# Down projections of a hybrid encoder: 16 of 22 row groups by a seven-product scheme, with the weights' split moved from POOL to ACT, DVE and POOL

## The reference

```python
def conv_ffn(x, w_up, conv_w, conv_b, w_down):
    hdn = x @ w_up                              # 1024 -> 2 x 2816
    hdn = causal_dwconv(hdn, conv_w, conv_b)    # 3 taps
    val, gate = jnp.split(hdn, [D_FF], axis=-1)
    return (jax.nn.gelu(gate) * val) @ w_down   # 2816 -> 1024
...
ff = conv_ffn(x, f_w_up[i], f_conv_w[i], f_conv_b[i], f_w_down[i])
x = layer_norm(ALPHA * x + ff, ln2_g[i], ln2_b[i])
```

## Time and profile before

| what | value |
|---|---|
| median of 3 runs (lowest to highest) | 1255.85 us (1255.59 to 1255.90) |
| span of the profiled execution | 1254.0 us |
| PE, PEld | 1246.9 us (99%), 1016.7 us (81%) |
| POOL, DVE, ACT | 861.5 us (69%), 551.0 us (44%), 410.2 us (33%) |
| loads of w_down | 44 of 512 KB, on SP's queue |
| down in layer 0 | from 500.75 us |

### The profile page before, as it was taken

How to read it: one execution, slowest core, us unless ns; L and a number is a source line. 1 busy time by engine, 2 the same in 40 slices (tenths; PEclk the granted TensorE clock), 3 DMA queues, 4 the chain that set the end, 5 groups by cost and what they waited for, 6 DMA issues and landing times.

```text
span 1254.0 us, 17715 instructions
## 1 busy us (share of the span) xinstructions
PE 1246.9 (99%) x5829; PEld 1016.7 (81%) x5829; DVE 551.0 (44%) x880; ACT 410.2 (33%) x684; POOL 861.5 (69%) x1154
## 2 busy tenths in 40 slices
PE   9999999999999999999999999999999999999998
PEld 6887777788888888888888778888888888888887
DVE  6556556564443444410444374364444443201352
ACT  4445444123434333100144484114343434100041
POOL 7555467629888777776577557929887787767573
PEclk9999999999999999999999999999999999999999
DMA  5221233303322233433143222312323224333221
GB/s 197 69 67 67 67 117 101 101 17 107 110 87 99 100 128 90 118 101 101 67 168 101 85 67 84 132 37 101 102 99 100 100 90 128 118 101 98 70 93 59
DMA packets 57292, 120.61 MB, mean 96 GB/s; under 512 B 3760, under 2 KB 36080, under 8 KB 56736
## 3 DMA queue, kind: packets, MB, share of 16 engines
q1 hardware_dynamic: 56192, 117.45, 28.8%
q10 hardware_dynamic: 1056, 2.58, 0.6%
HBM read 117.83 MB, written 2.20 MB: 96 GB/s over the span
## 4 chain that ended last, share of the span: by engine, by line
PE 97%; ACT 1%; DVE 1%; DMA 1%; issue 0%; DVEq 0%; ACTq 0%; SPq 0%
PE bank L439 19%; PE bank L440 19%; PE bank L441 19%; PE bank L458 9%; PE bank L459 8%; PE bank L460 8%; PE bank L735 2%; PE bank L740 2%; PE bank L733 2%; PE bank L554 1%; PE bank L541 1%; PE bank L467 1%; PE bank L525 1%; PE bank L523 1%; PE bank L909 1%; PE bank L910 1%
## 5 line engine op out<-in xcount | busy, mean ns | idle before, releaser
L425 POOL TENSOR_TENSOR w_lo<-stage,w_hi 128x256 fp32r<-128x256 f32 x800 | 593.8, 773 | 29.5 <-issue 1.5
L419 POOL TENSOR_SCALAR w_hi<-stage 128x1024 fp32r<-128x1024 f32 x200 | 213.8, 1069 | 172.8 <-PE bank L460 74.5
L439 PE MATMUL bank<-x_hi,w_hi 128*128 128x512 f32 (+1 forms) x712 | 275.7, 387 | 0.0
L441 PE MATMUL bank<-x_hi,w_lo 128*128 128x512 f32 (+1 forms) x712 | 275.3, 387 | 0.0
L440 PE MATMUL bank<-x_lo,w_hi 128*128 128x512 f32 (+1 forms) x712 | 275.3, 387 | 0.0
L439 PEld LDWEIGHTS bank<-x_hi,w_hi 128*128 128x128 f32 x712 | 133.7, 188 | 27.3
L441 PEld LDWEIGHTS bank<-x_hi,w_lo 128*128 128x128 f32 x712 | 133.7, 188 | 27.2
L440 PEld LDWEIGHTS bank<-x_lo,w_hi 128*128 128x128 f32 x712 | 133.7, 188 | 26.8
L1139 DVE SCALAR_TENSOR_TENSOR tmp<-bank,cols,tmp 128x511 f32<-128x511 f32 x88 | 66.0, 750 | 201.0 <-ACT tmp L1436 190.0
L458 PE MATMUL bank<-w_hi,h_hi 128*128 128x512 f32 x352 | 137.3, 390 | 0.0
L459 PE MATMUL bank<-w_lo,h_hi 128*128 128x512 f32 x352 | 137.0, 389 | 0.0
(11 more groups left out here) (180 smaller groups left out, 1804.6 us busy)
## 6 DMA issues: line engine op xcount, KB each, us to landing
stage<-w_square SPq DMA_DIRECT2D x163, 512.0 KB, 3.3
stage<-w_down SPq DMA_DIRECT2D x44, 512.0 KB, 3.7
rows<-norm_rows SPq DMA_DIRECT2D x4, 1024.0 KB, 5.7
outT<-x SPq DMA_DIRECT2D x7, 256.0 KB, 2.0
x<-xT SPq DMA_DIRECT2D x3, 512.0 KB, 6.8
p_in<-pT ACTq DMA_DIRECT2D x2, 512.0 KB, 3.2
w_ai<-w_lru SPq DMA_DIRECT2D x1, 1024.0 KB, 8.9
stage<-w_square ACTq DMA_DIRECT2D x1, 512.0 KB, 7.1
```

The costliest lines, as they stand in the source:

```text
L419: whole = pool.tensor_scalar(high[:, s, :], stage[:, s, :], 1.0, 0.0, ALU.mult, ALU.add)
L425: piece = pool.tensor_tensor(low[:, s, to], stage[:, s, to], high[:, s, to].bitcast(F32), ALU.subtract)
L439: pe.matmul(out, w_hi[:, s, c:c + P], m_hi, start=first, stop=False)
L441: return pe.matmul(out, w_lo[:, s, c:c + P], m_hi, start=False, stop=last)
```

## The change

`h` and the down weights are cut into 2 x 2 blocks: two halves of the tokens, pairs of row groups, two halves of the outputs. For 8 pairs (row groups 0 to 15) the four block products per output block (8 in all) are replaced by Strassen's scheme in the form with seven: three products in a first pass, four in a second, each over sums and differences of blocks. Row groups 16 to 21 go as before.

- **Sides of h** (DVE, in up): for rounds 0 to 7 the product of gelu and value goes to `folded`, with four sums per pair (`fold_sides`). In down ACT writes a side's high part (`side_top`), DVE its low part (`side_low`), 768 columns in a first-pass step and 1024 in a second-pass step, into three places (`JIT`).
- **Weights**: every unit of the 16 groups is loaded in both passes, through six places of `stage` (two of them on the dead `x_hi` and `x_lo`). DVE makes the sums in place (`first_sums`, `second_sums`), ACT the high part (`unit_top`), DVE the low part (`unit_low`); in the second pass POOL makes the low part of every second unit in four pieces (`near_low`). POOL splits the last six groups' units as before.
- **TensorE** (`fold_phase`): a product is 2 token tiles x 3 parts. A first-pass step has 3 products, a second-pass step 4, over all eight banks.
- **Results** (DVE): finished banks are added to x or taken from it (`block_fold`, 512 columns each, 20 per layer), and TensorE waits for that (`bank_folded`) before it takes the bank again.
- The convolution loops are unrolled on DVE and ACT, and the last round's second half is put between DVE's steps 2 to 5.

```diff
+            def fold_product(layer, step, r, part, pos, bank, first, last):
...
+                for tau in range(2):
+                    to = slice(tau * P, (tau + 1) * P)
+                    m_hi, m_lo = side_hi[step % JIT][:, pos, to], side_lo[step % JIT][:, pos, to]
+                    out = four(banks[bank + tau])
+                    pe.matmul(out, m_hi, high, start=first, stop=False, skip_group_check=True)
+                    pe.matmul(out, m_hi, low, start=False, stop=False, skip_group_check=True)
+                    mm = pe.matmul(out, m_lo, high, start=False, stop=last, skip_group_check=True)
...
+                for i in range(PRE):
+                    first, last, step, r = i == 0, i == PRE - 1, PRE + i, FOLD + 2 * i
+                    unit_ready(ph, 0, r)
+                    pe.wait_ge(side_ready, layer * 2 * PRE + step + 1)
+                    if first:
+                        pe.wait_ge(bank_folded, layer * 6 + 2)
+                    mm = fold_product(layer, step, r, 0, 1, 4, False, last)
...
+                    fold_product(layer, step, r, 1, 2, 6, False, last).then_inc(unit_used, 1)
+                    pe.wait_ge(near_split, layer * PRE + i + 1)
...
+                    mm = fold_product(layer, step, r + 1, 0, 0, 2, first, last)
...
+                    fold_product(layer, step, r + 1, 1, 3, 0, first, last).then_inc(unit_used, 1)
...
+            def near_low(layer, ph, i):
+
+                r = FOLD + 2 * i + 1
+                s = ph.slots[r] % SLOTS
+                pool.wait_ge(fold_high, layer * FOLD_UNITS + r + 1)
+                for c in range(0, UNIT, UNIT // PIECES):
...
+            def second_sums(layer, i):
+
+                r = FOLD + 2 * i
+                for n in (r, r + 1):
+                    dve.wait_ge(fold_loaded[fold_stage(n)], fold_fills(layer, n))
+                far, near = pair_of(staged(r)), pair_of(staged(r + 1))
+                dve.tensor_tensor(near[:, :, 0, :], near[:, :, 0, :], far[:, :, 0, :], ALU.add)
+                dve.drain()
+                dve.tensor_tensor(far[:, :, 0, :], near[:, :, 0, :], near[:, :, 1, :], ALU.add)
+                dve.drain()
+                dve.tensor_tensor(far[:, :, 1, :], far[:, :, 0, :], far[:, :, 1, :], ALU.add)\
+                    .then_inc(fold_summed, 1)
...
+            def unit_low(layer, r):
+
+                ph = phases[f"down{layer}"]
+                dve.wait_ge(fold_high, layer * FOLD_UNITS + r + 1)
...
+            def fold_down(layer):
...
+                for i in range(PRE):
+                    side_low(layer, i)
+                    if i + 1 < PRE:
+                        first_sums(layer, i + 1)
+                    else:
+                        second_sums(layer, 0)
+                    unit_low(layer, 2 * i)
+                    unit_low(layer, 2 * i + 1)
...
+                    r = FOLD + 2 * i
+                    side_low(layer, PRE + i)
+                    unit_low(layer, r)
+                    if i + 1 < PRE:
+                        second_sums(layer, i + 1)
+                    if i == 0:
+                        dve.wait_ge(unit_used, ph.done(0, FOLD - 2))
+                        for tau in range(2):
+                            folded_in = block_fold(2 + tau, 1, 6 + tau, True, False)
+                        folded_in.then_inc(bank_folded, 1)
+                        dve.wait_ge(product_done, layer * 3 + 1)
+                        for tau in range(2):
+                            folded_in = block_fold(tau, 0, 4 + tau, True, True)
+                        folded_in.then_inc(bank_folded, 1)
+                        dve.drain()
...
+            def side_top(layer, step):
+
+                ph = phases[f"down{layer}"]
+                if step >= JIT:
+                    act.wait_ge(unit_used, ph.done(0, 2 * (step - JIT) + 1))
+                elif step:
+                    act.wait_ge(unit_used, phases[f"up{layer}"].done(FT // 2 - 1, 3))
+                act.wait_ge(fold_sides_ready, layer * PRE + step % PRE + 1)
+                act.copy(side_part(side_hi, step), side_of(step)).then_inc(side_high, 1)
```

More of the change, by code:

```diff
@@ L133, in plan @@
     for name, slots, iters in want:
+        own = FOLD_UNITS if name.startswith("down") else 0
         last_used[SLOTS:] = [first - 1] * SLOTS
@@ L319, in rounds, with staged, pair_of, fold_fills @@
                     yield i
+        def staged(r):
+            s = fold_stage(r)
+            return stage[:, s, :] if s < SLOTS else stage_far[:, s - SLOTS, :]
+        def pair_of(unit):
+            return unit.rearrange("p (a b n) -> p a b n", a=4, b=2)
+        def fold_fills(layer, r):
+            s = fold_stage(r)
+            each = [fold_stage(n) for n in range(FOLD_UNITS)]
+            return 16 * (layer * each.count(s) + each[:r + 1].count(s))
+        def side_of(step):
+            return folded[:, step % PRE, 0:3, :] if step < PRE else folded[:, step % PRE, 3:7, :]
+        def side_part(tile, step):
+            return tile[step % JIT][:, 0:3 if step < PRE else 4, :]
         def one(t, m):
@@ L373, in _ @@
                     square_first += 2 * n
-                elif name != "rgx" and not name.startswith("down"):
+                elif name != "rgx":
                     square_first += ph.iters * n
@@ L796, in down_phase @@
                 ph = phases[f"down{layer}"]
[L797 to L809 removed]
+                fold_phase(layer)
@@ new lines, in conv_own @@
+            def conv_own(layer, i, half):
+                act.wait_ge(unit_used, phases[f"up{layer}"].done(i, half * 2 + 1))
+                act.wait_ge(h_lo_ready, i * 2 + (layer * FT + half + 1))
+                for part in (1, 0):
+                    r = half * 2 + part
+                    c = (i * 4 + r) * (CONV_F + 1) + COLS["conv", layer]
+                    act.activation(tmp[:, r, :], banks[r][:], ACT.Identity, bias=cols[:, c + 3:c + 4],
+                                   scale=cols[:, c + 2:c + 3]).then_inc(conv_first, 1)
@@ new lines, in conv_gelu, with h_high @@
+            def conv_gelu(layer, i, half):
+                act.wait_ge(conv_done, i * 4 + (layer * 2 * FT + half * 2 + 1))
+                act.activation(tmp[:, half * 2 + 1, :], tmp[:, half * 2 + 1, :],
+                               ACT.Gelu_apprx_tanh).then_inc(gelu_done, 1)
+            def h_high(layer, i, half):
+                k = (i - PRE) * 2 + half
+                act.wait_ge(h_ready, layer * REST + k + 1)
+                act.copy(h_hi[:, k, :], tmp[:, half * 2, :]).then_inc(h_hi_ready, 1)
```

352 lines of the change are left out of this document (274 added, 78 removed).

## The result

The changed kernel takes 1259.46 us (median of 8 runs, 1258.85 to 1260.25), the kernel before 1255.78 us beside it: a ratio of 1.0030, 95% interval 1.0021 to 1.0038. It is slower, by 3.7 us (0.3%); 1262 us was forecast, 1256 to 1269 as the forecast's own range.

A forecast was written before the change was run, and what follows sets the result against it. TensorE, busy 99% of the span, was taken to bound the kernel. Per layer 2.4 + 9.6 + 2.0 - 10.9 = +3.1 us, +6.2 in all, took the median of 1255.85 to 1262 us, range 1256 to 1269.

The forecast's parts named there:

- 48 matmuls removed: Down projection, per layer: 336 matmuls in place of 384, at 0.2267 us each, saves 10.9 us.
- first pass: Down's three-product steps: TensorE ends late behind DVE's queue and a late second side, +2.4 us on its own 32.6.
- between the passes and second pass: TensorE stands behind DVE's folds, then DVE's steps slowed by POOL take 6.3 us against 5.44: +9.6 us per layer.
- last six groups: End of down: POOL's units, 3.99 us each, start late and keep TensorE waiting, +2.0 us per layer, between 0.9 and 4.
- my clock: The forecast's time scale within a layer: zero is the first matmul of down, 500.75 in the earlier trace.
- some 5: Between the passes: TensorE was to stand for some 5 us behind the folds into x, going on at 40.3.
- The price of a meeting: Second pass: where POOL and DVE both read two SBUF tensors, each meeting was to cost DVE 0.6 us.
- The 0.5 that I took off 4 x 0.6: Second-pass step: about 0.5 us less than four full meetings, where a piece falls into DVE's drains and handoffs.
- The cover: Norm, ACT's copies, up's side sums, embedding input and decay rates were to stay beside TensorE's matmuls; counted at nothing.
- (1): Rival, chance 0.22: in the second pass's steps POOL and DVE pass each other; -4.0 us per layer, 1248 us.
- (2): Rival, chance 0.18: first pass too fast for its loads or DVE's starts, 1272 us; sign: TensorE's waits above 5 us.
- (3): Rival, chance 0.08: clock drops in the stand between passes, +5.4 us per layer, +2.0 net, 1266 us; sign: granted clock below 1.00.

The follow-up runs named there:

- Without the meetings: The changed kernel with POOL's low halves of every second unit in the second pass left out: 1251.19 us (0.9961 of the kernel before).
- the kernels with both edits: The changed kernel with DVE making every second-pass low half and the folds into x ahead of the sums: 1252.32 us (0.9968 of the kernel before).
- the one-piece kernel: The changed kernel with POOL making each second-pass low half as one piece of 1024 columns instead of four of 256: 1264.34 us (1.0069 of the kernel before).

## Why the prediction was right, point by point

The mechanism was right in each of the three terms: DVE's queue with POOL's pieces in it and POOL's units behind it. That the sum came within 2.5 us of the measured time is in part luck: two terms were 1 us too high per layer, one 0.6 too low, and inside them several sizes erred in opposite directions.

Measured in layer 0, from the first matmul of down at 500.72; layer 1 is 1.5 us in all as well.

| term, us per layer | forecast | measured |
|---|---|---|
| 48 matmuls removed | -10.9 | -10.9 |
| first pass | +2.4 | +1.4 |
| between the passes and second pass | +9.6 | +8.5 |
| last six groups | +2.0 | +2.6 |
| sum | +3.1 | +1.6 |

**The removed matmuls** are 96 by the page, and they come 0.227 us apart wherever the clock is full.

**First pass.** Its last matmul starts at 534.58, so that the pass takes 34.1 us instead of 32.6. The reason was right: the second step's side stood behind ACT's convolution, and with the convolution one step later the pass lost only 0.55 us (0.37 in layer 1). DVE's work from there took 28.5 us (503.13 to 531.67), 28.7 forecast. The size was off by 1: DVE's work began 2.41 us behind the start of down, not 2.84, so that TensorE was late by 0.54 us in the second step, not 1.2; and I had added 0.5 for starts behind a drain, which by these rows was not needed.

**Between the passes.** DVE's fourth fold ends at 540.27 and TensorE goes on at 540.42, 39.6 and 39.7 on my clock; 40.0 and 40.3 were forecast. The stand of 5.6 us is the "some 5" of the text, and so is its cause. But the moment came out right because two errors cancelled: DVE's queue came to this place 1 us earlier than I had it, and it met all four of POOL's pieces there (1.75, 1.22, 1.06 and 1.05 us), not two.

**Second pass.** The later steps of DVE take 6.25 us, 6.3 forecast; of the low halves of 1024 columns the sides' take 1.76, as said, the units' 1.21. The price of a meeting, 0.6, was too high. The two merged rows each begin with an operation that met POOL's high part of 1024 columns (511.96, 1.05 us, in the second), not a piece. Kept apart, the second row is:

```profile
512.18 1.36 DVE L1176 TENSOR_TENSOR p_lo<-p_in,p_hi 128x512 fp32r<-128x512 f32 x1 [3.92 <-ACT p_hi L1452]
513.47 1.22 DVE L1176 TENSOR_TENSOR p_lo<-p_in,p_hi 128x512 fp32r<-128x512 f32 x1
```

The operation that met pieces took 1.22 us, 0.53 more than alone. The 0.5 that I took off 4 x 0.6 made up for this: 1.9 charged, 1.7 measured. What failed is the number of such steps: I charged 6.3 us to all six and 3.2 to the last, from 41.4 on my clock. The first two took 5.3 and 5.9 us (541.56, 546.89, 552.75), because POOL had no piece to do from 543.76 to 549.09, and the last low half ended at 580.64, 79.9 on my clock, not 82.4. The term was mis-sized by 1.1: of the measured 8.5, the stand is 5.6, the slow matmuls 1.8, and later waits and starts 1.0. I had also expected waits of about 0.9 us on POOL's pieces in each of the later steps. They did not come: there is one per layer, 0.5 and 0.2 us, because the slow matmuls and the two shorter steps had put DVE ahead.

**Last six groups.** POOL's chain was as described, 3.99 us a unit as in the earlier trace rows; its lateness was some 0.6 us more than taken, because one unit (592.49, 3.53 us for its pieces in the trace of after, 2.83 alone) met the embedding's operations.

**The cover.** I counted the decay rates and the embedding's input at nothing. In the changed kernel that held, but only just: the matmul behind the norm (615.16) starts 0.2 us late. As soon as the chain ahead of them grew shorter, they became the next wait, 2.8 us. I had named the cover, but not how thin it was.

**The rivals.** (1) POOL and DVE don't pass each other. Without the meetings 1251 us is measured, where I gave 1248. Of the difference 2.0 us are again that cover; the rest is in the second pass, 5.5 and 6.5 us above TensorE's own time where I gave 4.1, since matmuls ran slow behind the stand there too. (2) The loads were not late: from 505 to 510 the DMA engines were busy 98% of the time and moved 307 GB/s, and still DVE waited for a load only 0.2 us in the first pass, and TensorE was 1.4 us late in all, not the 5 that I gave as the sign. The tile's loads:

```profile
DMA to landing us min/median/max: 3.5/4.3/7.2
```

The median load took 4.3 us, 3.7 in the earlier trace rows. (3) The clock did drop, so that the sign that I gave for this rival came, but for 9 matmuls and 1.8 us (11 and 2.3 in layer 1), less than the 5.4 that I priced. In this kernel it cost next to nothing: TensorE had DVE's slower steps to wait for anyway, which was the reason that the rival itself gave for taking most of it back. The warning of the Trainium skill, page "TensorE: Matmul & The Clock Gate", section "HAM oscillation — how this bites in real kernels", about idle gaps in front of matmuls agrees with that stand. The stands of 1.7 us in the kernels with both edits had no slow matmuls behind them.

**The size of a meeting.** The rule of the Trainium skill, page "SBUF — State Buffer", section "Who interferes with whom", that the later of two such instructions blocks for the whole of the earlier, agrees with the one-piece kernel (2.90 us in place of 0.69). My reading of it, a whole piece per meeting and 6.7 us a step, doesn't: with four pieces a meeting cost 0.38 to 0.54 us. That a part of each piece passes while DVE starts its next operation is my reading of the difference, and not shown. The same section says that a DVE instruction with at most one input in SBUF, outside DVE's two-port modes, doesn't contend with GpSimd. The trace agrees: the folds, which read x and a bank, took 0.68 us beside POOL's pieces at 583 to 587 us, as they do alone.

## What to carry to other kernels

When work is taken off an engine, sum up the queue that now feeds it, from its first late operation to its last, and ask which single chain ends the phase: a long wait on the relieved engine beside such a chain is not a cost, and removing it only moves it. A helper engine whose operations hold up those of the engine it helps gives nothing when the operations it saves are shorter than the meetings it makes: here 1.14 us saved cost 1.7. And a cover that costs nothing should be written down with its width, since every gain ahead of it uses it up.

## What the runs showed of the hardware

- DVE operations with both inputs in SBUF and POOL's subtractions of two SBUF tensors hold each other up, and the runs look as if they took turns, operation by operation: against 4.55 us a step without POOL, one piece cost DVE 2.2 us, four pieces 1.7, eight pieces 0.9, but then POOL, alone 0.42 us a piece, needs 1.0 us each.
- After a stand of 5.6 us TensorE ran nine matmuls at 1.2 GHz in one layer and eleven in the other. After stands of 1.7 us none was slow. After stands of 2.2 us, in two of the kernels, none was slow in layer 0 and some were in layer 1: stands of much the same length don't always end alike.
